# A decoder trunk's expert stage: last quad written out, last units in halves, first tokens without a gather

## What is computed

```python
h = rms_norm(x, norm_ffn_g[layer])
g_idx = argmax(h @ w_group + b_group)              # one of 4 groups for each token
top_v, top_i = top_k(e_logits of that group, 2)    # two of its 4 experts
top_w = softmax(top_v) * g_w
for each expert e, over the tokens xb that chose it:
    y = (silu(xb @ w_gate[e]) * (xb @ w_up[e])) @ w_down[e]     # three 1024x1024 matrices
x = x + sum of top_w * y over the two experts of a token
```

## Time and profile before

| | us |
|---|---|
| median of 3 runs (1140.05 to 1140.25) | 1140.24 |
| the profiled execution | 1141.35 |
| its span (first to last instruction) | 1139.6 |
| PE busy | 1102.1 (97% of the span) |
| DVE busy | 453.2 (40%) |
| ACT busy | 200.8 (18%) |
| DMA, mean rate over the span | 385 GB/s |
| layer 0's expert stage, first expert product to last | 146.98 to 570.97 |
| layer 1's expert stage | 708.54 to 1132.51 |

### The profile page before, as it was taken

How to read it: one execution, slowest core, us unless ns; L and a number is a source line. 1 busy time by engine, 2 the same in 40 slices (tenths; PEclk the granted TensorE clock), 3 DMA queues, 4 the chain that set the end, 5 groups by cost and what they waited for, 6 DMA issues and landing times.

```text
span 1139.6 us, 13479 instructions
## 1 busy us (share of the span) xinstructions
PE 1102.1 (97%) x5416; PEld 503.0 (44%) x5416; DVE 453.2 (40%) x804; ACT 200.8 (18%) x380; POOL 6.4 (1%) x29
## 2 busy tenths in 40 slices
PE   7999999999999999999999999999999999999997
PEld 5887633333333333333368775333333333333332
DVE  5875542222332233222286785233223322222223
ACT  4565200000000000000074561000000000000001
POOL 2000000000000000000000000000000000000000
PEclk9999999999999999999999999999999999999999
DMA  9756999999999999999993669999999999999996
GB/s 344 216 206 254 392 389 427 428 427 428 429 428 429 428 428 427 430 428 429 417 387 138 248 242 390 394 429 426 429 427 429 428 428 430 428 430 427 429 428 261
DMA packets 53838, 439.13 MB, mean 385 GB/s; under 512 B 12080, under 2 KB 12080, under 8 KB 29232
## 3 DMA queue, kind: packets, MB, share of 16 engines
q1 hardware_dynamic: 53520, 438.72, 93.0%
q10 hardware_dynamic: 288, 0.00, 0.0%
HBM read 437.66 MB, written 1.05 MB: 385 GB/s over the span
## 4 chain that ended last, share of the span: by engine, by line
PE 83%; DMA 9%; DVE 4%; SPq 2%; ACT 1%; issue 0%; ACTq 0%; DVEq 0%
PE bank L1963 51%; DMA ring<-in_moe_w_up 9%; PE bank L1793 7%; PE bank L1975 5%; PE bank L1939 4%; PE bank L1821 4%; PE bank L1798 2%; SPq L531 2%; PE bank L1948 1%; PE bank L2006 1%; PE bank L1743 1%; PE bank L1999 1%; PE bank L1623 1%; DMA ring<-in_ab_w_in 1%; DVE work L1371 1%; PE bank L1573 1%
## 5 line engine op out<-in xcount | busy, mean ns | idle before, releaser
L1963 PE MATMUL bank<-ring,work 128*64 128x512 f32 x2304 | 513.7, 594 | 12.6 <-DVE work L1502 6.3
L1963 PEld LDWEIGHTS bank<-ring,work 128*64 128x64 f32 x2304 | 161.6, 137 | 344.9 <-issue 326.4
L1492 DVE TENSOR_SCALAR work<-work 128x512 f32<-128x512 f32 x32 | 13.7, 427 | 455.7 <-ACT work L967 455.7
L970 ACT ACTIVATE attention<-bank 128x512 f32<-128x512 f32 x32 | 19.1, 597 | 531.7 <-PE bank L1963 531.7
L1494 DVE RECIPROCAL work<-work 128x512 f32<-128x512 f32 x32 | 107.3, 3353 | 1.1
L1499 DVE TENSOR_TENSOR work<-bank,work 128x512 f32<-128x512 f32 x32 | 22.1, 692 | 113.6 <-PE bank L1963 113.6
L1939 PE MATMUL bank<-x_sb,root_y 128*64 128x512 f32 x272 | 64.2, 593 | 0.0
L1793 PE MATMUL bank<-rounded,h_high 128*128 128x512 f32 x256 | 62.3, 395 | 0.0
L967 ACT ACTIVATE work<-bank 128x512 f32<-128x512 f32 x32 | 19.1, 597 | 227.5 <-PE bank L1963 227.5
L1963 PE MATMUL bank<-ring_over_v,work 128*64 128x512 f32 x256 | 57.7, 593 | 1.3 <-DMA ring_over_v<-in_moe_w_gate 1.3
L1963 PE MATMUL bank<-ring_over_qk,work 128*64 128x512 f32 x256 | 57.6, 592 | 0.0
(11 more groups left out here) (245 smaller groups left out, 901.4 us busy)
## 6 DMA issues: line engine op xcount, KB each, us to landing
ring<-in_moe_w_up SPq DMA_DIRECT2D x64, 2048.0 KB, 29.3
ring<-in_moe_w_gate SPq DMA_DIRECT2D x48, 2048.0 KB, 28.0
ring<-in_moe_w_down SPq DMA_DIRECT2D x32, 2048.0 KB, 27.9
ring_over_qk<-in_moe_w_down SPq DMA_DIRECT2D x16, 2048.0 KB, 27.7
ring_over_v<-in_moe_w_gate SPq DMA_DIRECT2D x16, 2048.0 KB, 29.0
ring_spare<-in_moe_w_down SPq DMA_DIRECT2D x16, 2048.0 KB, 31.0
ring<-in_ab_w_in SPq DMA_DIRECT2D x12, 1024.0 KB, 13.6
ring<-in_c_w_in SPq DMA_DIRECT2D x12, 1024.0 KB, 14.4
```

The lines of the kernel that those rows point to most:

```text
L1963: last = mm(b[SLOTS * half:SLOTS * (half + 1), :], left(h, k), expert_rhs(slot, k, half), start=(h == 0 and k == 0), stop=(h == 1 and k == ...
```

## The change

1. **The last quad is written out.** `Fori(0, last_quad)` runs one quad fewer on PE, ACT and DVE, then `expert` stands three times and `last_expert` once, in straight code. (SP's loop was already made so.)
2. **The last expert is ordered otherwise.** No gather, copy, transposes and tables for an expert that does not exist. The scatter of the expert before and the transposes of `give` (into MISC) come between gate and up. hid is multiplied, transposed (into GATE and MISC) and copied by pairs of chunks: pair 0 is hid's columns 0 and 1 of each four, pair 1 the columns 2 and 3. Down begins when pair 0 is there; its chunk 2 waits for pair 1.
3. **The last three units of a layer (up 3, down 4 and 5) are loaded in two halves** of 1024 KB, pieces of 8 KB, the first raising `half_loaded`. PE's chunks 0 and 1 of the unit wait for the first half, chunks 2 and 3 for the second.
4. **First expert's tokens.** `first_tokens` multiplies pieces of x (128 tokens x 128 features, stationary, every fourth column) with the table (64 columns, moving), which gives the tokens gathered and transposed at once, chunks 0 and 1 in GATE, 2 and 3 in MISC; DVE multiplies each pair with the gain (`leave_first_tokens`). For every first unit of an expert gate's chunk 2 has its own wait, on the second count of `xt_ready`. `take_ready` is raised for each half of the table. `residual(3)` is split: half of its columns before the wait on `chosen`, half after the ranks.
5. **Layer 1's first weights:** `first_half` exists for each layer, and ACT rounds the first half of the unit when that half has landed (before: when both had).
6. Semaphores are shared or merged (`max_ready`, `moe_out`, `o_sumsq`, `forget_abs`); counts are adapted.

The diff, cut to its core:

```diff
@@ load_unit_by_halves, SP
+            def load_unit_by_halves(layer, slot, u, e):
+                w = (moe_w_gate, moe_w_up, moe_w_down)[u // 2][layer]
+                src = w[e:e + 1].rearrange("e (h p s) n -> (e h) p (s n)", h=2, s=SUB)[u % 2]
+                for part in range(2):
+                    cols = slice(UNIT // 2 * part, UNIT // 2 * (part + 1))
+                    sp.dma_start(ring[slot][:, cols], src[:, cols]).then_inc(
+                        layers[layer].unit_loaded[slot] if part else half_loaded[u - HALVED], 16)
...
-                    load_unit(layer, slot, i % UNITS, N_EXPERTS - QUAD + i // UNITS)
+                    if i < QUAD_UNITS - UNITS + HALVED:
+                        load_unit(layer, slot, i % UNITS, N_EXPERTS - QUAD + i // UNITS)
+                    else:
+                        load_unit_by_halves(layer, slot, i % UNITS, N_EXPERTS - 1)
@@ weights_high, ACT
-                act.wait_ge(s.unit_loaded[WIN_SLOTS[layer][u]], win_loaded(layer, u))
+                if u == 0 and layer > 0 and halves[0] == 0:
+                    act.wait_ge(first_half[layer], 16)
+                else:
+                    act.wait_ge(s.unit_loaded[WIN_SLOTS[layer][u]], win_loaded(layer, u))
@@ DVE
+            def leave_first_tokens(layer):
+                g = gain_ffn[:, layer, :].rearrange("p (h s a) -> p s h a", h=2, a=1)
+                for pair in range(2):
+                    chunks_of = slice(2 * pair, 2 * pair + 2)
+                    dve.wait_ge(layers[layer].xt_psum, pair + 1)
+                    tt(xT[:, chunks_of, :, :],
+                       (GATE, MISC)[pair][:, T * pair:T * (pair + 1)].rearrange(
+                           "p (s h t) -> p s h t", s=2, h=2),
+                       g[:, chunks_of].to_broadcast([P, 2, 2, SLOTS]), ALU.mult
+                       ).then_inc(layers[layer].xt_ready, 1)
...
+                def last_expert(quad, k):
+                    silu(quad, k)
+                    dve.wait_ge(s.giveT_psum, turns(quad, k + 1))
+                    nc.vector.tensor_copy(giveT[k % 2][:, :], MISC[:, 0:T]
+                                          ).then_inc(s.giveT_ready, 1)
+                    dve.wait_ge(*used(layer, quad, k, 3))
+                    for pair in range(2):
+                        tt(chunk_pair(hid, pair), chunk_pair(UP[:, :], pair), chunk_pair(sig, pair),
+                           ALU.mult).then_inc(s.hid_ready, 1)
+                    for pair in range(2):
+                        dve.wait_ge(s.hidT_psum, turns(quad, k + 1 + pair))
+                        nc.vector.tensor_copy(
+                            hidT[:, 2 * pair:2 * pair + 2, :],
+                            (GATE, MISC)[pair][:, T * pair:T * (pair + 1)].rearrange(
+                                "p (s t) -> p s t", s=2)
+                            ).then_inc(s.hidT_ready, 1)
@@ PE
+                def first_tokens():
+                    for pair in range(2):
+                        for c in (2 * pair, 2 * pair + 1):
+                            for h in range(2):
+                                at = P * c + SLOTS * h
+                                for t in range(NT):
+                                    if c == 0 and h == 0:
+                                        pe.wait_ge(s.take_ready, t + 1)
+                                    last = mm((GATE, MISC)[pair][:, at:at + SLOTS],
+                                              by_chunk(x_sb, t, h, c), take[:, t, :],
+                                              start=(t == 0), stop=(t == NT - 1))
+                        last.then_inc(s.xt_psum, 1)
...
-                gather(1)
-                tokens_out(1)
+                first_tokens()
...
+                def last_expert(quad, k):
+                    gated(quad, k)
+                    scatter(turns(quad, k), k - 1)
+                    give_across(MISC, turns(quad, k + 1))
+                    two_halves(UP, tokens, quad, k, (2, 3), halved=(3,))
+                    for pair in range(2):
+                        pe.wait_ge(s.hid_ready, turns(quad, k + 1 + pair))
+                        hidden_across((GATE, MISC)[pair], (2 * pair, 2 * pair + 1))
+                    pe.wait_ge(s.hidT_ready, turns(quad, k + 1))
+                    two_halves(Y, hidden, quad, k, (4, 5), (s.hidT_ready, turns(quad, k + 2)),
+                               halved=(4, 5))
+                    scatter(turns(quad, k + 1), k)
+
+                with pe.Fori(0, last_quad) as quad:
...
+                for k in range(QUAD - 1):
+                    expert(last_quad, k)
+                last_expert(last_quad, QUAD - 1)
```

More of the change, by code:

```diff
@@ L406, in win_loaded @@
         def win_loaded(layer, u):
[L408 removed]
+            return 16 if u == 0 else 32
         def by_columns(slot):
@@ L1508, in _ @@
+                with dve.Fori(0, last_quad) as quad:
+                    for k in range(QUAD):
+                        expert(quad, k)
+                for k in range(QUAD - 1):
+                    expert(last_quad, k)
+                last_expert(last_quad, QUAD - 1)
                 for q in range(2):
@@ new lines, in tokens, with hidden, give_across @@
+                def tokens(h, c):
+                    return xT[:, c, h, :]
+                def hidden(h, c):
+                    return hidT[:, c, SLOTS * h:SLOTS * (h + 1)]
+                def give_across(b, count):
+                    pe.wait_ge(s.give_ready, count)
+                    for t in range(NT):
+                        last = nc.tensor.transpose(b[:, P * t:P * (t + 1)], give[:, t, :],
+                                                   ident[:, :])
+                    last.then_inc(s.giveT_psum, 1)
@@ new lines, in hidden_across, with gated @@
+                def hidden_across(b, chunks):
+                    for c in chunks:
+                        part = hid.rearrange("p (q s) -> p s q", s=SUB)[:, c, :]
+                        last = nc.tensor.transpose(b[:, P * c:P * (c + 1)], part, ident[:, :])
+                    last.then_inc(s.hidT_psum, 1)
+                def gated(quad, k):
+                    pe.wait_ge(s.xt_ready, quad * (2 * QUAD) + (2 * k + 1))
+                    if k >= 1:
+                        pe.wait_ge(s.giveT_ready, turns(quad, k))
+                    two_halves(GATE, tokens, quad, k, (0, 1),
+                               (s.xt_ready, quad * (2 * QUAD) + (2 * k + 2)))
@@ new lines, in expert @@
+                def expert(quad, k):
+                    now, after = turns(quad, k + 1), turns(quad, k + 2)
+                    gated(quad, k)
+                    gather(after)
+                    two_halves(UP, tokens, quad, k, (2, 3))
+                    pe.wait_ge(s.gate_act, now)
+                    give_across(GATE, now)
+                    tokens_out(after)
+                    pe.wait_ge(s.hid_ready, now)
+                    hidden_across(UP, range(SUB))
+                    if k >= 1:
+                        scatter(turns(quad, k), k - 1)
+                    pe.wait_ge(s.hidT_ready, now)
+                    two_halves(Y, hidden, quad, k, (4, 5))
```

175 lines of the change are left out of this document (86 added, 89 removed).

## The result

The changed kernel takes **1145.93 us**, the median of 5 runs (1145.11 to 1147.30). The kernel before, run beside it, has 1140.24 (5 runs, 1139.99 to 1140.89). The ratio is 1.0048, 95% interval 1.0036 to 1.0059: **5.7 us slower**, where 5.0 us faster was forecast, and outside the range.

The account below looks back on a forecast made before the run. Expert weight loads were taken to bound each layer's end, PE layer 1 up to its experts. Per layer 0.2 us at the first expert plus 2.3 at the last, 5.0 in all: 1140.24 to 1135.2 us, range 1133.6 to 1138.0.

Parts of the forecast that it names:

- First expert's tokens: Before each layer's first expert: 32 load-product pairs at 0.122 us, 3.9 us in all; 0.2 us gained per layer.
- No term below depends on: Granted clock is full, 2.4 GHz, in all four stretches read, so no forecast term depends on it.
- value_load: PE's read of the quad count behind the first expert's narrow products: 0.25 us exposed, between 0 and 0.54.
- better head: Rival at the first expert: pairs at 0.11 us, quad-count read hidden; 0.8 us gained per layer, 1134.0 us; chance 0.12.
- The tail: Each layer's last expert: reordering and halved loads let down end at 1130.2 instead of 1132.5, 2.3 us gained.
- Landings: Last expert's units: first halves land 2.45 us sooner, last landing at 1128.2; down waits for landings inside a unit.
- Carry-over: Layer 1's start: its first product comes 2.3 us earlier; the rival without this has 1137.5 us, chance 0.08.
- The written-out block: Rival at each layer's loop exit, about 464 us: PE stalls on instructions; a 10 us stall gives 1147.2 us; chance 0.04.
- worse head: Rival at the first expert: pairs at 0.145 us, quad-count read exposed; 0.8 us lost per layer, 1137.2 us; chance 0.11.

Follow-up runs that it names:

- mended form: The changed kernel with ScalarE copying x so each piece has neighbouring columns, which the narrow products read: 1134.85 us against 1140.59 for the kernel before.
- the head alone: The changed kernel with its last quad back in the loop and whole units, narrow first-token products kept: 1150.66 us, ratio 1.0080 to the kernel before.
- the experiment with the late wait: The changed kernel with the old head, ScalarE also waiting for both halves of layer 1's first weights: 1139.50 us, 0.9993 of the kernel before.

## Why the prediction was wrong

**The failed step** is the price of a pair in "First expert's tokens": "64 columns lie between; I take 0.122", with ends of 0.11 and 0.145. It came from two rows, one of which had contiguous pieces (four loads before 20 columns) and the other the right distance but transposes. Neither had both properties of the new instruction, an ordinary f32 product on columns 16 bytes apart. It measures 0.24. With the distance taken away it is 0.116; with the kind changed to an ordinary product the transposes' loads take 329 ns too. I interpolated over the number of moving columns, as if these made the difference between the two rows. The distance was in the second row but hidden by its kind. The trace of before could have told: transposes load in 141 ns from neighbouring columns and in 211 from x. Put on the 190 ns of L1919's loads, that ratio gives 190 x 211 / 141 = 284 ns, an estimate; it is still short of the 329 measured, but far above the 211 on which my upper end of 0.145 stood.

**"No term below depends on" the clock** failed too. The statement was read from stretches of wide products, and the change puts narrow ones in their place. The granted clock fell to 0.50 in each head and made gate 1.44 and 1.11 us longer. Of the 11.1 us between the change and its mended form the pace is 2 x (7.66 - 3.74) = 7.8 and the clock 2.6; 0.7 is left over. How much the clock costs differs between executions: gate lost 1.9 us in each layer of the head alone.

**value_load** was put at 0.25 exposed. In the change gate's first load starts 0.12 us behind the last narrow one (149.29 and 149.17), so nearly nothing of it is exposed. With the pace mended the head gains 0.8 per layer, which is the rival "better head", not the forecast's 0.2.

**The tail** was right in nearly every row: 2.2 us against 2.3 forecast; down starts at 14.69 instead of 14.57. DVE's halves take 0.62 each instead of 0.5 (median of the four of L1556; the two overlap, 1.14 together). A multiplication of as many neighbouring columns takes 0.42 (L1401 in the same trace). Bank, `sig` and `hid` are all strided in L1556, so which of the three costs the 0.2 is not shown. Landings played less than I had written: in the change's trace the weight load of the last half unit waits for its landing in both layers (0.62 us idle, 0.57 in layer 1, against 0.28 between other loads), but PE's products run on, 3.60 us for the unit as before. In layer 0 the wait makes the tail 1.5 us longer with contiguous pieces, and 0.35 with every second column; otherwise the halves do their part by being there in time.

**Carry-over** was right, and the experiment with the late wait shows its mechanism: 2.4 us where 2.3 were forecast.

**The written-out block** does not stall PE. Instruction packets in one queue rose from 20 to 28 and nothing on PE waits for them: from the last looped quad's scatter (465.96) to the next gate (467.88) are 1.92 us, and 1.92 before (462.19 to 464.11).

```profile
q8 instruction: 28, 0.46, 0.2%
```

The rival that ended slower was this one, for which nothing was found. The mechanism that made it slower was in the rival "worse head", at a size that I had excluded: with 0.24 in place of 0.145 its own sum gives 3.9 us lost per layer, and 3.3 with nothing of the value_load exposed. Measured are 3.15 before the clock, because the first product starts 0.17 us before the tables end. The forecast of 1135.2 us is nearly what the change does with its pieces side by side, 1134.85, but that is in part luck: it gains 5.7 us, not 5.0, since the head gives four times what was forecast.

## What to carry to other kernels

Price a new instruction from a row that has its kind *and* its access pattern, not from two rows with one of them each. Where no row has both, look for a pair of rows of one kind that differ in the pattern alone, and carry their ratio over; here even that fell short (284 against 329 ns), so let the upper end be twice the load. Before reading a stationary operand across columns, look at the distance of its numbers: 8 bytes cost nothing here, at 16 bytes a pair took twice as long. An idle engine can lay the data out (eight copies a layer on ScalarE turned 5.7 us lost into 5.7 us gained). And a run of narrow products in place of wide ones puts the clock into the sum, the products after it included: the clock fell where they ran for 7.7 and 5.8 us and stayed full where they ran for 3.8.

## What was not expected of the hardware

- An f32 weight load of 128 columns in an ordinary product: 192 ns for neighbours, 196 for every second column, 329 for every fourth. In a transpose: 141 for neighbours, 211 for every fourth.
- The granted clock at half level does not slow those strided loads: they are 308 to 330 ns in the changed kernel, across both levels, and 308 to 332 with the clock at 0.999.
- ScalarE pays for the same distance, it seems: its copies of 256 columns 16 bytes apart take 0.64 to 0.68 us, as long as its squares of 512 neighbouring columns (0.63). No run separates the distance from the rest.
- The old head can lose the clock too, 1.7 us a time: in both layers of one trace and in one layer of another, both of kernels that have the new last expert beside the old head.
